# Placing the expert-row work of a two-layer hybrid trunk by a table instead of by even weights

## What is computed

```python
best, pos = lax.top_k(cand, PEER_TOPK)
idx = jnp.take_along_axis(cand_idx, pos, axis=-1).reshape(t, PEER_HEADS * PEER_TOPK)
gate = jax.nn.softmax(best, axis=-1).reshape(t, PEER_HEADS * PEER_TOPK)
act = jax.nn.gelu(jnp.einsum('ted,td->te', jnp.take(u_tab, ib, axis=0), xb), approximate=False)
w = (gb * act).astype(x.dtype)
return jnp.einsum('te,ted->td', w, jnp.take(v_tab, ib, axis=0))
```

## Time and profile before

| | |
|---|---|
| time, median of 3 runs | 3287.8 us (3285.88 to 3300.96) |
| profiled execution: its time, its span | 3323.2 us, 3321.4 us |
| mean granted TensorE clock | 0.787 of full |
| moved by DMA | 959.26 MB, mean 289 GB/s |
| of it by the gathers (q0) | 805.40 MB |
| unit 1, unit 2, unit 3, tail | from 382, 1046, 1904 and 2571 us |

### The profile page before, as it was taken

The page is one execution under the profiler, slowest core; times in us unless marked ns, Lnnn a source line. Parts: engine busy times, 40 slices in busy tenths (PEclk is TensorE's granted clock), DMA queues, the critical chain, the costliest instruction groups (busy, mean ns, idle before and its releaser), DMA issues.

```text
span 3321.4 us, 27774 instructions
## 1 busy us (share of the span) xinstructions
PE 1944.2 (59%) x10194; PEld 1140.6 (34%) x10194; DVE 1769.2 (53%) x3951; ACT 360.2 (11%) x801; POOL 1725.5 (52%) x1540
## 2 busy tenths in 40 slices
PE   5888476657873321348878684676892000057787
PEld 4667365544642311331233163562660000001111
DVE  2423688862178988960013388873149888830000
ACT  2222111102111000000010011111210000000000
POOL 0000374434344777876545574444342877766665
PEclk9879687767996555679989996777896555579999
DMA  7557495546886998899999897546784999999998
GB/s 288 178 183 315 156 393 178 178 141 239 290 292 229 370 411 283 301 320 367 361 334 365 299 353 259 178 152 214 252 319 148 336 367 367 379 358 366 355 364 317
DMA packets 249064, 959.26 MB, mean 289 GB/s; under 512 B 32353, under 2 KB 33505, under 8 KB 231137
## 3 DMA queue, kind: packets, MB, share of 16 engines
q0 software_dynamic: 221184, 805.40, 66.9%
q1 hardware_dynamic: 19584, 142.62, 11.4%
q10 hardware_dynamic: 8160, 9.46, 0.8%
HBM read 955.01 MB, written 2.36 MB: 288 GB/s over the span
## 4 chain that ended last, share of the span: by engine, by line
POOL 25%; PE 25%; DVE 21%; DMA 13%; issue 13%; ACT 3%; ACTq 1%; another core or an unknown queue 0%; POOLq 0%; DVEq 0%
POOL sb_ring L486 25%; PE pb L509 16%; DMA sb_ring<-in_peer_v,sb_idxT 10%; PE pv L509 7%; DVE sb_ring L1803 6%; DMA sb_ring<-in_peer_u,sb_idxu 2%; PE pb L512 1%; DVE sb_pos L1715 1%; ACT sb_big L989 1%; DVE sb_big L1710 1%; ACT sb_hT L989 1%; DVE sb_big L1502 1%; DVE sb_big L1374 1%; DVE sb_big L1521 1%; DVE sb_big L1762 1%
## 5 line engine op out<-in xcount | busy, mean ns | idle before, releaser
L486 POOL DMA_INDIRECT sb_ring<-in_peer_u,sb_idxu x768 | 980.5, 1277 | 861.5 <-PE pv L509 399.1
L486 POOL DMA_INDIRECT sb_ring<-in_peer_v,sb_idxT x768 | 744.7, 970 | 714.9 <-PE pv L509 464.6
L1803 DVE CUSTOM_DVE_ANT_0 sb_ring<-sb_ring,sb_h 128x1024 f32<-128x1024 f32 x768 | 916.3, 1222 | 141.3 <-DMA sb_ring<-in_peer_u,sb_idxu 108.4
L509 PE MATMUL pv<-sb_ring,sb_wcol 128*32 128x512 f32 x3072 | 754.9, 646 | 174.4 <-DMA sb_ring<-in_peer_v,sb_idxT 139.6
L509 PE MATMUL pb<-sb_hT,sb_wring 128*128 128x256 f32 (+1 forms) x1920 | 383.7, 361 | 106.5 <-ACT sb_cinP L989 62.3
L509 PEld LDWEIGHTS pb<-sb_hT,sb_wring 128*128 128x128 f32 x1920 | 328.8, 207 | 180.8 <-issue 72.4
L509 PEld LDWEIGHTS pv<-sb_ring,sb_wcol 128*32 128x32 f32 x3072 | 134.5, 114 | 732.8 <-DMA sb_ring<-in_peer_v,sb_idxT 501.2
L509 PE MATMUL pb<-sb_big 128*128 128x128 f32 (+2 forms) x1888 | 257.4, 308 | 114.9 <-DVE sb_big L1502 80.6
L509 PEld LDWEIGHTS pb<-sb_big 128*128 128x128 f32 (+1 forms) x1888 | 250.4, 218 | 126.8 <-DVE sb_big L1502 85.6
L512 PE MATMUL pb<-sb_cst,sb_dots 128*128 128x128 f32 x6 | 2.7, 452 | 397.3 <-DVE sb_dots L1809 393.3
L1816 DVE COPY sb_accv<-pv 128x1024 f32<-128x1024 f32 x6 | 7.3, 1225 | 386.9 <-PE pv L509 373.7
(11 more groups left out here) (219 smaller groups left out, 1816.9 us busy)
## 6 DMA issues: line engine op xcount, KB each, us to landing
sb_wring<-in_w_in_blocks SPq DMA_DIRECT2D x32, 1024.0 KB
sb_ring<-in_w_mod_blocks SPq DMA_DIRECT2D x30, 1024.0 KB, 5.1
sb_wring<-in_w_q_blocks SPq DMA_DIRECT2D x27, 1024.0 KB
sb_wring<-in_w_mod_blocks SPq DMA_DIRECT2D x18, 1024.0 KB
sb_wring<-in_w_out_blocks SPq DMA_DIRECT2D x13, 1024.0 KB
sb_ring<-in_peer_u,sb_idxu POOLq DMA_INDIRECT x768
sb_ring<-in_peer_v,sb_idxT POOLq DMA_INDIRECT x768
sb_ring<-in_w_in_blocks SPq DMA_DIRECT2D x8, 1024.0 KB, 6.2
```

The source lines that it names most:

```text
L486: pool.indirect_dma_start(ring[:, j, :], None, a["tab_" + kind][l_of(q)], bass.IndirectOffsetOnAxis(ap=of, axis=0)).then_inc(rows_in[j], 16)
L509: return nc.tensor.matmul(out, lhsT, rhs, start=start, stop=stop)
L1803: dve.tensor_tensor_reduce(out=ring[:, j, :], in0=ring[:, j, :], in1=h2[:, t, :], scale=1.0, scalar=0.0, op0=ALU.mult, op1=ALU.add, accum_ ...
```

## The change

Three things. A u item becomes two rows (UB = 2), so a tile has 64 of them; v items stay at four rows. In units 1 and 3 the proportional spread is replaced by a table (woven), which says for each point how many u items and v items run there. And the first 8 u items (16 rows) of the unit's own first tile (q 1 in unit 1, q 4 in unit 3), which before could start only in the next unit, run in topk1. In unit 2 the proportional spread stays, with a u item counted as half a v item and 8 items fewer.

The table in units 1 and 3, as rows: 

| where | u rows before | u rows now | v items before | v items now |
|---|---|---|---|---|
| norm1 | 4 | 0 | | |
| proj | 52 | 32 (16 at points 2 to 9, 16 at its end) | | |
| scal, pre | 12 | 26 | | |
| intra0, intra1 | 56, in fours at 7 of 11 points | 56, in twos and fours at every point | | |
| scan | 4 | 14 (8 at its end) | 5 | 0 |
| fnet, attp | | | 2 | 6 |
| att0, att1 | | | 4 | 8 |
| out | | | 4 | 8 |
| query | | | 10 | 10, all from point 7 on |
| topk0, topk1 | | 16 of the next tile (topk1) | 7 | 0 |

```diff
--- before.py
+++ after.py
@@ -52,6 +52,7 @@
 
 HB = 4
 STEP = 2 * HB
+UB = 2
 STEPS = SLOTS // STEP
 
 
@@ -156,11 +157,25 @@
     return [k for k, _ in mix_points(u) if isinstance(k, str)]
 
 
+def woven(u, point):
+
+    stage, k = point if isinstance(point, tuple) else (point, None)
+    if k is None:
+        products = {"proj": 8, "scal": 2, "pre": 4, "intra0": 1, "intra1": 1, "scan": 4}
+        sums = {"fnet": 2, "attp": 2, "att0": 1, "att1": 1}
+    else:
+        products = {"proj": int(2 <= k < 10), "scal": 2, "pre": 3, "intra0": 1 + (k in (0, 2, 9)), "intra1": 1 + (k in (0, 2, 9)),
+                    "scan": int(k < 3)}
+        sums = {"attp": 2, "att0": 1, "att1": 1, "out": 1, "query": int(k >= 7)}
+    return products.get(stage, 0), sums.get(stage, 0), int(k is not None and stage == "topk1" and k < 8)
+
+
 def schedule():
 
 
     main = [("const",), ("layer", 0)]
     side, upto = [], {}
+    begun, begun_by = {}, (1, 3)
     for u in range(len(UNITS)):
         if u == 0:
             own = [("modblocks", 0, k, k + 1) for k in range(8, 24)] + [("modsum", 0, 1)]
@@ -168,21 +183,46 @@
         else:
             own = []
             for q, t in seq_tiles(u - 1):
-                own += [("u", q, t, i, i + 1, (h,)) for i in range(STEPS) for h in range(2)]
+                own += [("u", q, t, i, i + 1, (h,)) for i in range(STEPS) for h in range(STEP // UB)][begun.get(q, 0):]
+            products = list(own)
             for q, t in seq_tiles(u - 1):
                 own += [("gelu", q, t)] + [("v", q, t, i, i + 1, (h,)) for i in range(STEPS) for h in range(2)] + [("end", u - 1, q, t)]
         pts = mix_points(u)
         if u == 0:
             first = [n for n, (k, _) in enumerate(pts) if k == "proj"][0]
             pts = [(k, w if n > first else 0) for n, (k, w) in enumerate(pts)]
-        total, steps, past, n = sum(w for _, w in pts), sum(it[0] in ("u", "v", "modblocks") for it in own), 0, 0
+        if u in begun_by:
+            q, t = seq_tiles(u)[0]
+            first = [("u", q, t, i, i + 1, (h,)) for i in range(STEPS) for h in range(STEP // UB)]
+            own = list(products)
+            sums = [("v", seq_tiles(u - 1)[0][0], 0, i, i + 1, (h,)) for i in range(STEPS) for h in range(2)]
+            nu = nv = ns = 0
+            own += [("gelu", *seq_tiles(u - 1)[0])] + sums + [("end", u - 1, *seq_tiles(u - 1)[0])]
+            for k, _ in mix_points(u):
+                a, b, c = woven(u, k)
+                nu, nv, ns = nu + a, nv + b, ns + c
+                n = nu + (k == "scan" or nv > 0) + nv + (nv == len(sums) and (ns > 0 or k in ("query", "topk0", "topk1")))
+                upto[u, k] = len(side) + n + ns
+            assert nu == len(products) and nv == len(sums)
+            begun[q] = ns
+            own += first[:ns]
+            side += own
+            for st in stages_of(u):
+                if st == "load" and u == 2:
+                    main.append(("layer", 1))
+                main.append(("mix", st, u))
+            main.append(("drain", u))
+            upto[u, "drain"] = len(side)
+            continue
+        cost = {"u": UB / HB, "v": 1, "modblocks": 1}
+        total, steps, past, n = sum(w for _, w in pts), sum(cost.get(it[0], 0) for it in own), 0, 0
         for k, w in pts:
             past += w
-            ran = sum(it[0] in ("u", "v", "modblocks") for it in own[:n])
-            while n < len(own) and (own[n][0] not in ("u", "v", "modblocks") or ran + 1 <= past / total * steps + 1e-6):
+            ran = sum(cost.get(it[0], 0) for it in own[:n])
+            while n < len(own) and (own[n][0] not in cost or ran + cost[own[n][0]] <= past / total * steps + 1e-6):
                 if own[n][0] in ("gelu", "end", "modsum") and not isinstance(k, str):
                     break
-                ran += own[n][0] in ("u", "v", "modblocks")
+                ran += cost.get(own[n][0], 0)
                 n += 1
             upto[u, k] = len(side) + n
         side += own
@@ -195,7 +235,8 @@
         main.append(("drain", u))
         upto[u, "drain"] = len(side)
     for q, t in seq_tiles(3):
-        main.append(("u", q, t, 0, STEPS, (0, 1)))
+        for n in range(begun.get(q, 0), STEPS * STEP // UB):
+            main.append(("u", q, t, n // (STEP // UB), n // (STEP // UB) + 1, (n % (STEP // UB),)))
     for q, t in seq_tiles(3):
         main += [("gelu", q, t), ("v", q, t, 0, STEPS, (0, 1)), ("end", 3, q, t)]
     main.append(("final",))
@@ -1797,7 +1838,7 @@
                         dve.wait_ge(*done("h2_copied", (u, [x for x, _ in seq_tiles(u)].index(q), k)))
                 for i in range(i0, i1):
                     for h in halves:
-                        for j in range(h * HB, h * HB + HB):
+                        for j in range(h * UB, h * UB + UB):
                             k = i * STEP + j
                             dve.wait_ge(rows_in[j], 16 * (rows_before(p) + i + 1))
                             dve.tensor_tensor_reduce(out=ring[:, j, :], in0=ring[:, j, :], in1=h2[:, t, :], scale=1.0, scalar=0.0,
```

## The result

The changed kernel takes 3338.9 us (median of 4 runs, 3333.0 to 3352.1), and the kernel before, run beside it, 3292.1 us: ratio 1.0127, 95% interval 1.0084 to 1.0169. It is 47 us slower. Forecast were 3277 us and a range that ended at 3320.

What follows compares the result with a forecast made beforehand. No engine was busy over 59%, so the bound was taken to change by stage. Units 1 and 3 at +18 each, unit 2 -24 and tail -23 sum to -11 us: 3287.8 becomes 3277, range 3235 to 3320.

Steps and rivals of the forecast that it cites:

- Terms 1 to 4: Unit 1's u part: proj -15 us, scal and pre +14, both chunk stages together -11, scan +2.
- Term 5: Unit 1, scan to attention: five v items leave, two products come before the gelu; -16 us (-8 to -20).
- Term 6: Unit 1, fnet to out: 22 v items instead of 15, transfers bind by a little; +27 us (+15 to +45).
- the rival in which rows and mixer work alternate: Attention and out: TensorE waits for v rows at nearly every item; term 6 +45, total +25, 3313 us; chance 0.13.
- term 7: Unit 1, query: ten v items in both kernels, eight rows ahead at point 7; 0 us (-3 to +10).
- term 8: Unit 1, end: 6.6 us between last top-k step and first product become about 5 at query's end; -1 us.
- Term 9: Unit 1, topk1: 16 products on VectorE with nothing to hide them and no idle time; +18 us.
- Term 10: Unit 2: 16 u rows fewer, taken at 1.5 us each; -24 us (0 to -28).
- Term 11: Tail: 16 rows at 1.43 us each saved; -23 us, called the surest term.
- The rival of starved runs: Units 1 and 3: long product runs slow gathers, 16 rows at 1.14 us more, 18 us each; 3313 us; chance 0.07.

Runs made afterwards that it cites:

- the v table: Against the kernel before, only the v items go by the table; products stand where they stood, no own products: 1.0123, 3341.5 us.
- the product table: Against the kernel before, only the products of u rows go by the table; v items stand at their old points, no own products: 0.9984, 3288.1 us.

## Why the prediction was wrong

The sum was -11 us; the medians say +47. By its own steps, in unit 1 (unit 3 is told below), from the profiles of the change against before:

- **Terms 1 to 4** (proj, scal and pre, chunk stages, scan): predicted -15, +14, -11, +2. Measured -19 with norm1, +16, -13, +3: -12 where -10 was said. Right, down to the level of 7.1 us. Only the credit was misplaced: the spread in twos gives -9 in unit 1 without any table.
- **Term 5** (scan to attention): predicted -16. The stretch fell from 35.3 to 19.3 us: right. The five items that left it stand in term 6, which counted them.
- **Term 6** (v rows from fnet to out) failed: +27 predicted, +39.5 measured (101.4 to 140.9 us from the first attention step to norm). The mechanism was the one the forecast named, transfers bind, and so were its counts; the rate was off. It put the last half block's end 120 us behind the first attention step, the trace 134 (747.2 to 881.3). Until the last row came that this block had to wait for (747 to 876), the trace moved 40.86 MB of v rows, 78 rows' worth where 76 were counted, and three weight blocks:

```profile
DMA packets 11662, 44.11 MB, mean 342 GB/s; under 512 B 1296, under 2 KB 1296, under 8 KB 11271
q0 software_dynamic: 11223, 40.86, 86.1%
q1 hardware_dynamic: 432, 3.15, 6.4%
L527 POOL DMA_INDIRECT sb_ring<-in_peer_v,sb_idxT x80 | 75.3, 941 | 54.8 <-PE pv L550 35.3 <-issue 19.5
L550 PE MATMUL pv<-sb_ring,sb_wcol 128*32 128x512 f32 x330 | 70.0, 617 | 18.5 <-DMA sb_ring<-in_peer_v,sb_idxT 17.1 <-ACT sb_solW L1030 1.1
```

At 1.43 us a row and 8.5 for the blocks that would be 118 us; at the 342 GB/s that the stretch really got it was 129, and behind the last row stood 5.5 us of TensorE's work where 2 were counted. The transfers didn't run at full rate throughout (share 0.93): in this stretch POOL waited 35.3 us for TensorE to free places in the ring, and TensorE waited 17.1 us for rows. So it comes close to the rival in which rows and mixer work alternate, and to its price of +45. That rival's total of +25 was still short, by term 7 and unit 2. This growth is the v table's alone: from the first attention step to norm it is 139.2 us with the v table, 139.3 with both tables (no own products) and 99.2 with the product table. What the product table costs lies ahead of that step, where terms 4 and 5 (-14, measured -12.5) had it.
- **Term 7** (query: 0, at most +10) failed: norm and query grew by 17 us, 12 of them for the items, 5 for the end item, which left top-k (-5.5, in the kernel without own products), so that **term 8** (-1) was right. "Eight rows are ahead at point 7" was true and too little. No gather is issued in norm (DMA share 0.37) and the seven half blocks ahead of the first item; the ten items behind them need 40 rows. Spreading them gave those 12 us back in each unit.
- **Term 9** (own products in top-k): +18 predicted, 17.6 measured between the kernels with and without them.
- **Term 10** (unit 2: -24) looked confirmed by the two profiles, 852.3 to 828.9. The second profile of before shows 839.2, and the kernels with and without own products differ by 8 us. The -24 fitted one pair of executions; the second pair gives -11.
- **Term 11** (tail: -23): from the start of unit 3's top-k to the end, the second profiles differ by -8.6 us, with +12 of top-k in it: -21, and 16 rows at 1.29 us are 21.

The second profiles of both kernels, taken when the tail's rows came equally fast, add up without a remainder: unit 1 +40.8, unit 2 -11.2, unit 3 up to its top-k +22.8, top-k and tail -8.6, the rest -0.2: 43.6 us, the difference of their spans (3284.7 and 3328.3). Forecast were +18 for unit 1 and +18 for unit 3, measured +41 and +35. Terms 6 and 7 carry most of it, with some 12 us a unit each more than forecast (the end item's 5 in query apart, which top-k gives back); unit 2, at -11 instead of -24, adds 13. The v table is the cause, shown by undoing it alone (1.0132 to 0.9984) and by moving seven of its items and spreading query's (1.0122 to 0.9916).

The rival of starved runs had the same sign and its sum was +25. The gathers do issue slowly beside products, 1.68 to 1.99 us instead of 0.94, in the change too:

```profile
491.74 1.68 POOL L527 DMA_INDIRECT sb_ring<-in_peer_u,sb_idxu  x1 [2.08 <-DVE sb_dots L1844]
493.73 1.99 POOL L527 DMA_INDIRECT sb_ring<-in_peer_u,sb_idxu  x1 [0.31 <-issue]
496.02 0.94 POOL L527 DMA_INDIRECT sb_ring<-in_peer_u,sb_idxu  x1 [0.30 <-issue]
```

In direction this agrees with the Trainium skill, SBUF — State Buffer, section SBUF: two separate sides, by which an operation with two SBUF inputs keeps GpSimd's reads out. But VectorE waited only 9.8 us for u rows in the whole u part, and the product table alone is no slower than before: here the ring of eight rows covers it, and the rule moves nothing.

Not tried: v items of fewer than four rows, a ring of more than eight rows, and other seats for the end item.

## What to carry to other kernels

Price a moved item by the stretch it lands in, from its first to its last dependent work, at the rate that the transfers will get there with this ring, waits for its places included, and add the work that stands behind the last row; a place where transfers stand still just ahead of one where they bind is a loss of its own. The v items that hid under another engine's long stage (top-k) cost nothing that could be measured there, and 4 us each in out, so look first for what leaves such a place. A unit of work should be small enough to fill a wait exactly: three inverse levels held eight products in the time of six, and only items of one could be spread so.

Take a second profile of the kernel before when a term rests on rates of a transfer-bound stretch.

## What the runs showed of the hardware

The rate of the tail's u rows differs between executions: the kernel before moved one row per 1.41 us in its first profile and one per 1.29 in its second. Over all fourteen profiles it is 1.29 to 1.32 in six and 1.35 to 1.45 in eight, in a stretch where nothing but gathers runs; the v rows behind it took 1.44 to 1.46 in each. Over some 250 rows this is 30 us, as much as a change here is worth, and it explains most of why the first profiles agree to 10 us where medians differ by 47. What sets it was not found.
